# Fused transformer block and mixture of experts: expert weights in DMA runs of four and three slots, and two small reorderings

## The chip, the cores and the metric

The kernel runs on one core of one Trainium2 chip. A NeuronCore has TensorE (PE, matrix products, with weight loads shown apart as PEld), VectorE (DVE), ScalarE (ACT), GpSimd (POOL) and SyncE (SP), which here issues all the DMAs. The metric is the time on the device of one launch, in microseconds, lower is better.

## What is computed

Two blocks follow each other on 256 tokens of width 1024, all in float32. The first has two kinds of attention, a causal depthwise convolution in a gated feed-forward part (width 2816) and a gated embedding. The second has a modulation of its inputs by a condition vector, a convolution, a sparse attention, a pooling mixer and then a mixture of 32 experts. Cut to what the change touches:

```python
h = rms_norm(x, g_pre_ffn[i])
u = causal_depthwise_conv(h @ w_up[i], conv_w[i], conv_b[i])
gate, val = jnp.split(u, 2, axis=-1)
f = (jax.nn.gelu(gate, approximate=True) * val) @ w_down[i]
...
mod = cond @ mod_w[l] + mod_b[l]                     # second block
...
def run(args):                                       # one expert, its tokens
    tok, e = args
    hb = hf[tok]
    return (jax.nn.silu(hb @ w1[e]) * (hb @ w3[e])) @ w2[e]
```

All 32 experts' matrices are read from HBM whatever tokens chose them: each expert has w1, w3 (1024 x 512 each) and w2 (512 x 1024), 6 MB in float32.

## The kernel before

**Weights and the ring.** All large weights pass through `ring`, seven slots of 4096 float32 in each of 128 partitions (2 MB a slot). `STREAM` lists the loads in their order, `PLACE` gives each its slot, round robin in the expert stage, and `BEFORE` names the load that held the slot before. SP walks the stream in that order; ahead of a load it waits (`used`) until the last reader of the old content is done. SP waits in order, so a load that waits holds back those behind it.

**The expert stage.** The experts go in eight groups of four. In a group the four experts stand beside each other in the partitions (32 rows each), so a group has 12 slots of weights: slots 0 to 7 are w1 and w3 (PE products that read `sq`), slots 8 to 11 are w2 (products that read `ar`). Load `j` is slot `j % 12` of group `j // 12`. After slot 7 PE gathers part of the next group's tokens, transposes, and waits for ACT and DVE; after slot 11 DVE takes the result out, PE adds it to the tokens' sums and gathers the rest of the next group's tokens before slot 0 can begin. After group 2, PE also spreads one more row for the end of the kernel.

**Runs.** `RUNS` joins neighbouring loads into one DMA, whose row in a partition is as long as all of them together. From load 19 on the kernel before has runs of two, two and three: loads 19, 21 (two), 23 (three), 26, 28 (two), 30 (three), and so on up to 89 (two), then 91 and 92 singly, and the last ones in parts. A run of two at place 3 (loads 26 + 7i) fills slots 3 and 4, one at place 5 (loads 28 + 7i) slots 5 and 6, and one of three at place 0 (loads 23 + 7i) slots 0 to 2. A run is issued when all of its slots are free, and has one landing: `loaded` gives PE the landing of the whole run for any slot of it.

**The up stage.** `w_up` comes in eleven slabs `j` of eight chunks `k` (512 columns of a partition). Each chunk is split into a rounded part (`hi`, made by ACT) and the rest (`lo`, by DVE, or by POOL for k = 3 and 7), and PE takes 12 products of it. Chunk buffers are four, so ACT can make chunk k when PE has finished chunk k - 4. Between the chunks of slab j, the slab before it is convolved and gated (`conv_step`): ACT makes the base (steps 3 and 4) and the gelu (5), DVE the taps, POOL the product (8), then ACT the product's `hi` and POOL its `lo` (step 9). Step 9 of slab j - 2 stands behind chunk 1 of slab j on ACT and behind chunk 0 on POOL.

**The down stage.** `w_down` is taken in 44 steps in the same way, with the `hi` part on ACT and the `lo` part on DVE. Between these, DVE does one `mod_column` after each of the twelve steps of `DOWN_COLUMNS`, a product and sum of 1024 elements (line 162) with the modulation weights, independent of `w_down`.

Of the kernel before, what the change touches and what calls it, by code (L numbers as in the profile page):

```python
# [57 lines left out]
BEFORE = {x: y for i, x in enumerate(STREAM) for y in [z for z in STREAM[:i] if PLACE[z] == PLACE[x]][-1:]}  # L58


RUNS = {19: 2}
for _i in range(10):
    RUNS.update({21 + 7 * _i: 2, 23 + 7 * _i: 3, 26 + 7 * _i: 2})
RUN_OF = {j: next((a for a in RUNS if a <= j < a + RUNS[a]), j) for j in range(3 * NE)}


# [102 lines left out]
def build(nc, A, out):  # L169
    with ExitStack() as ctx:  # L170
# [61 lines left out]
        def slot(name, j):  # L232
            i = PLACE[name, j]
            return ring[:, i * SLOT:(i + 1) * SLOT]
# [5 lines left out]
        def expert_rows(j):  # L240

            n = RUNS.get(RUN_OF[j], 1)
            o = (j - RUN_OF[j]) * SLOT
            if n == 1:
                return A["exps"][[i for i in range(3 * NE) if RUN_OF[i] not in RUNS].index(j)]
            return A[f"exps{n}"][[i for i in RUNS if RUNS[i] == n].index(RUN_OF[j])][:, o:o + SLOT]

        def expert_run(j):
            n = RUNS[j]
            return A[f"exps{n}"][[i for i in RUNS if RUNS[i] == n].index(j)]  # L250
# [82 lines left out]
        def weight_place(n):  # L333

            buf, o = (fr, WP + 1024 * (n % 4)) if n % 4 < 2 else (fr_h, 1024 * (n % 4 - 2))
            return buf[:, o:o + 512], buf[:, o + 512:o + 1024]
# [10 lines left out]
        def down_src(f, n):  # L347
            return slot("wdown", f // 4)[:, (f % 4) * 1024 + 512 * n:(f % 4) * 1024 + 512 * n + 512]
# [937 lines left out]
        def scalar(act):  # L1286
# [193 lines left out]
            def up_rounded(j, k):  # L1480
                act.wait_ge(loaded("wup", j), pe_up[(8 * j + k - 4) // 8, (k - 4) % 8] if 8 * j + k > 3 else None)
                weight_rounded(8 * j + k, slot("wup", j)[:, 512 * k:512 * k + 512], act_up, "hi", j, k)
# [64 lines left out]
            def conv_step(j, step):  # L1547
                if step == 3:
                    conv_base(j, 0)
                elif step == 4:  # L1550
                    conv_base(j, 1)
                elif step == 5:
                    act.wait_ge(dve_up["conv", j, 0])
                    act.activation(conv_place(j, 0), conv_place(j, 0), ACT.Gelu_apprx_tanh).then_inc(act_up, "gelu", j)
                elif step == 9:
                    act.wait_ge(pool_up["f", j])
                    act.copy(fr[:, FH + 512 * j:FH + 512 * j + 512], conv_place(j, 0)).then_inc(act_up, "f_hi", j)

            for j in range(1, 11):
                for k in range(5 if j == 1 else 0, 8):  # L1560
                    up_rounded(j, k)
                    if j == 1:
                        conv_step(0, k - 2)
                    else:
                        conv_step(j - 1, k)
                        if k == 1:
                            conv_step(j - 2, 9)


# [237 lines left out]
        def vector(dve):  # L1807
# [63 lines left out]
            def mod_column(i):  # L1871

                j, o = i // 4, 1024 * (i % 4)
                dve.wait_ge(loaded("modw", j), act_mod["crow", int(i > 3)])
                if i > 0:
                    dve.wait_ge(dve_mod["column", i - 1])
                t = dve.products_sum(sq[:, 1024:2048], slot("modw", j)[:, o:o + 1024], sq[:, 0:1024], mod[:, i:i + 1]).then_inc(dve_mod, "column", i)
                if i == 15:
                    dve.wait_ge(t)
                    dve.tensor_tensor(mod[:, 0:16], mod[:, 0:16], col("mod_b", 0, 16), ALU.add).then_inc(dve_mod, "first")  # L1880
# [212 lines left out]
                    input_rest(k - 1)  # L2093
            up_rest(0, 7)

            DOWN_COLUMNS = (13, 15, 18, 20, 23, 25, 28, 30, 33, 35, 38, 40)


            def conv_tap(j, p, d):
# [32 lines left out]
            for i, (f, n) in enumerate(DOWN_ORDER):  # L2132
                hi, lo = weight_place(i)
                dve.wait_ge(act_down["hi", f, n])
                dve.tensor_tensor(lo, down_src(f, n), hi.bitcast(F32), ALU.subtract).then_inc(dve_down, "lo", f, n)
                if i in DOWN_COLUMNS:
                    mod_column(4 + DOWN_COLUMNS.index(i))
                if i == 4:
# [285 lines left out]
        def gpsimd(pool):  # L2424
# [34 lines left out]
            def rest(signal, key, src, hi, lo, t, ready):  # L2459
                pool.wait_ge(t, ready)  # L2460
                return pool.tensor_tensor(lo, src, hi.bitcast(F32), ALU.subtract).then_inc(signal, *key)
# [16 lines left out]
            for j in range(1, 11):  # L2478
                for k in range(8):
                    if ("lo", j, k) in POOL_UP:  # L2480
                        t = rest(pool_up, ("lo", j, k), slot("wup", j)[:, 512 * k:512 * k + 512], *weight_place(8 * j + k), t,
                                 act_up["hi", j, k])
                    if j > 1 and k == 0:
                        t = conv_step(j - 2, 9, t)
                t = conv_step(j - 1, 8, t)
            t = conv_step(9, 9, t)
# [359 lines left out]
        @block.scalar  # L2846
        def _(e):
            p = Program(e)
            scalar(p)
            when_flagged(p, over_scalar)  # L2850

        @block.gpsimd
        def _(e):
            gpsimd(Program(e))
# [137 lines left out]
```

## Time and profile before

| what | value |
|---|---|
| median of 3 runs | 911.45 us (911.08 to 913.74) |
| the profiled execution | 911.76 us |
| its span, first to last instruction | 910.0 us |
| PE busy | 757.1 us, 83% of the span |
| DVE busy | 414.5 us, 46% |
| ACT busy | 337.4 us, 37% |
| share of the chain that ended last | PE 51%, DMA 31%, DVE 12% |
| moved by DMA | 299.01 MB, of which the expert weights are 201 MB (96 slots) |

The page divides the span into 40 slices of 22.75 us. Up to slice 23 the PE row shows 9 in each; then, in the expert stage, it falls to 4 to 7 and the DMA row rises to 9 in each. "Chain that ended last" follows the last instruction back through what released it; it tells which engine the time belongs to, but a DMA's share in it includes the time that the DMA stood behind another in the queue.

### The profile page before, as it was taken

The page shows a single profiled execution, that of the slowest core. Times are in us where ns is not written, and L with a number is a line of the kernel's source. Part 1 is how long each engine was busy: PE and PEld are TensorE (multiplying, and loading weights), DVE is VectorE, ACT ScalarE, POOL GpSimd, SP SyncE. Part 2 cuts the span into 40 slices and gives each one's busy share as a digit, 9 for nine tenths or more (in the row PEclk, how much of TensorE's full clock was granted, in tenths as well). Part 3 has the DMA queues.
Part 4 walks back from the last instruction along what each step waited for, and adds up shares of the span by engine and source line. Part 5 has one row for each costly group of instructions (what it writes and reads, how often), then busy time and mean ns, then how long its engine had stood idle before and what let it go on. Part 6 is the DMA issues. An engine that isn't in the chain of part 4 may idle for free.

```text
span 910.0 us, 12726 instructions
## 1 busy us (share of the span) xinstructions
PE 757.1 (83%) x5292; PEld 524.8 (58%) x5292; DVE 414.5 (46%) x851; ACT 337.4 (37%) x664; POOL 136.5 (15%) x136
## 2 busy tenths in 40 slices
PE   9999999999999999999999984567574575665575
PEld 7986589999998877898786431123221222212223
DVE  5777777899998975899613110010100100001002
ACT  5766667666666667824723110001000000000012
POOL 0011043544431334103010000000000000000000
PEclk9999999999999999999999997789888888888888
DMA  9958964455553982646968999999999999999995
GB/s 352 423 209 315 427 243 162 185 186 185 186 185 108 387 340 79 266 175 236 341 256 328 431 444 424 427 433 431 432 428 431 435 432 429 431 442 418 433 423 242
DMA packets 19648, 299.01 MB, mean 329 GB/s; under 512 B 2176, under 2 KB 2560, under 8 KB 6144
## 3 DMA queue, kind: packets, MB, share of 16 engines
q1 hardware_dynamic: 19584, 298.13, 79.9%
q8 instruction: 43, 0.70, 0.3%
q14 instruction: 21, 0.17, 0.1%
HBM read 297.08 MB, written 1.05 MB: 328 GB/s over the span
## 4 chain that ended last, share of the span: by engine, by line
PE 51%; DMA 31%; DVE 12%; ACT 4%; issue 1%; POOL 0%; SPq 0%; DVEq 0%; POOLq 0%
PE ps L114 51%; DMA ring<-in_exps 31%; DVE ar L140 3%; DVE fr L132 2%; DVE sq L162 1%; DVE fr_h L132 1%; DVE yT L140 1%; ACT L120 1%; ACT yT L120 1%; PE ps L117 1%; DVE hT L140 0%; DVE ar L132 0%; ACT ar L123 0%; ACT sq L120 0%; ACT ar L120 0%
## 5 line engine op out<-in xcount | busy, mean ns | idle before, releaser
L114 PE MATMUL ps<-fr 128*128 128x256 f32 (+2 forms) x1332 | 213.3, 316 | 1.6 <-DVE fr L132 0.8
L114 PEld LDWEIGHTS ps<-fr 128*128 128x128 f32 (+1 forms) x1332 | 187.3, 189 | 21.0 <-DVE fr L132 2.7
L114 PE MATMUL ps<-ring,sq 128*32 128x512 f32 x936 | 127.6, 697 | 78.3 <-DMA ring<-in_exps 78.3
L114 PE MATMUL ps<-ring,ar 128*32 128x512 f32 (+4 forms) x784 | 87.8, 573 | 52.4 <-DMA ring<-in_exps 48.4
L114 PEld LDWEIGHTS ps<-ring,sq 128*32 128x32 f32 x936 | 31.4, 125 | 165.6 <-DMA ring<-in_exps 91.9
L132 DVE TENSOR_TENSOR ar<-ar,ps 128x512 f32<-128x512 f32 x9 | 6.2, 688 | 241.5 <-PE ps L114 240.2
L132 DVE TENSOR_TENSOR fr<-ring,fr 128x512 fp32r<-128x512 f32 (+2 forms) x119 | 92.5, 804 | 12.0 <-ACT fr L123 11.7
L123 ACT ACTIVATE fr<-ring 128x512 fp32r<-128x512 f32 (+2 forms) x143 | 84.7, 623 | 33.5 <-PE ps L114 30.4
L114 PEld LDWEIGHTS ps<-ring,ar 128*32 128x32 f32 (+1 forms) x784 | 26.3, 120 | 99.6 <-issue 45.6
L123 ACT ACTIVATE ar<-ps 128x512 f32<-128x512 f32 (+4 forms) x48 | 27.2, 570 | 151.8 <-PE ps L117 131.4
L132 DVE TENSOR_TENSOR ar<-ps,ar 128x512 f32<-128x512 f32 (+6 forms) x38 | 23.4, 632 | 120.7 <-PE ps L114 120.4
L120 ACT ACTIVATE sq<-ps,misc 128x128 f32<-128x128 f32 x31 | 11.9, 456 | 162.7 <-PE ps L114 162.7
L114 PE MATMUL ps<-fr,fr_h 128*128 128x256 f32 x552 | 70.6, 284 | 0.1
L114 PE MATMUL ps<-ar 128*128 128x512 f32 (+10 forms) x328 | 62.3, 407 | 8.1 <-DVE ar L132 6.9
L114 PEld LDWEIGHTS ps<-fr,fr_h 128*128 128x128 f32 x552 | 67.5, 191 | 0.6 <-DVE fr_h L132 0.3
L132 POOL TENSOR_TENSOR ar<-ar 128x128 f32<-128x128 f32 (+2 forms) x21 | 11.2, 533 | 309.7 <-DVE ar L132 308.6
L114 PEld LDWEIGHTS ps<-ar 128*128 128x128 f32 (+4 forms) x328 | 35.5, 168 | 36.9 <-issue 16.7
L123 ACT ACTIVATE fr_h<-ring 128x512 fp32r<-128x512 f32 x66 | 41.5, 633 | 22.2 <-PE ps L114 22.1
L132 DVE TENSOR_TENSOR fr_h<-ring,fr_h 128x512 fp32r<-128x512 f32 x43 | 46.2, 1083 | 6.8 <-ACT fr_h L123 6.6
L120 ACT ACTIVATE ar<-ps 128x768 f32<-128x768 f32 (+1 forms) x21 | 14.8, 715 | 84.8 <-PE ps L114 83.4
L132 POOL TENSOR_TENSOR fr<-ring,fr 128x512 fp32r<-128x512 f32 x24 | 34.1, 1421 | 66.2 <-ACT fr L123 65.3
L140 DVE SCALAR_TENSOR_TENSOR yT<-ps,cols,yT 128x255 f32<-128x255 f32 (+1 forms) x88 | 37.2, 475 | 4.6 <-ACT yT L120 4.6
(193 smaller groups left out, 918.0 us busy)
## 6 DMA issues: line engine op xcount, KB each, us to landing
ring<-in_exps SPq DMA_DIRECT2D x21, 4096.0 KB, 28.5
ring<-in_exps SPq DMA_DIRECT2D x10, 6144.0 KB, 26.9
ring<-in_modw SPq DMA_DIRECT2D x12, 2048.0 KB, 8.9
ring<-in_exps SPq DMA_DIRECT2D x12, 2048.0 KB, 10.1
ring<-in_wup SPq DMA_DIRECT2D x11, 2048.0 KB, 12.3
ring<-in_wdown SPq DMA_DIRECT2D x5, 2048.0 KB, 7.9
ring<-in_win SPq DMA_DIRECT2D x4, 2048.0 KB, 11.8
ring<-in_exps SPq DMA_DIRECT2D x8, 1024.0 KB, 10.4
```

The lines of the kernel that those rows point to most:

```text
L114: return Issue(self.e and self.e.matmul(o, l, r, start=start, stop=stop, skip_group_check=True))
L117: return Issue(self.e and self.e.transpose(o, i, ident))
L120: return Issue(self.e and self.e.activation(o, i, f, **kw))
L123: return Issue(self.e and self.e.activation(o, i, ACT.Copy, scale=scale))
L132: return Issue(self.e and self.e.tensor_tensor(o, a, b, op))
L140: return Issue(self.e and self.e.scalar_tensor_tensor(out=o, in0=a, scalar=s, in1=b, op0=op0, op1=op1))
L162: return Issue(self.e and self.e.tensor_tensor_reduce(out=o, in0=a, in1=b, scale=1.0, scalar=0.0, op0=ALU.mult, op1=ALU.add, accum_out=total))
```

## The change

Three edits:

1. `RUNS`: loads 19, 21 and 23 stay as they are (two, two, three). From load 26 on, the two runs of two become one run of four (26 + 7i, slots 3 to 6), nine times, between the runs of three (30 + 7i, slots 0 to 2). The last run of two (89) and all that is behind it stay. Row length of a run of four is 64 KiB in a partition, and its array in HBM is laid out for it.
2. Step 9 of slab 0 (the product's `hi` on ACT and `lo` on POOL), in slab 2 alone, stands behind chunk 3 instead of chunk 1 (ACT) and chunk 0 (POOL).
3. Three of the twelve `mod_column` stand at other steps of the down stage: 13 becomes 14, 15 becomes 16, 38 becomes 37.

```diff
-RUNS = {19: 2}
-for _i in range(10):
-    RUNS.update({21 + 7 * _i: 2, 23 + 7 * _i: 3, 26 + 7 * _i: 2})
+RUNS = {19: 2, 21: 2, 23: 3, 89: 2}
+for _i in range(9):
+    RUNS.update({26 + 7 * _i: 4, 30 + 7 * _i: 3})
...
                         conv_step(j - 1, k)
-                        if k == 1:
+                        if k == (3 if j == 2 else 1):
                             conv_step(j - 2, 9)
...
-            DOWN_COLUMNS = (13, 15, 18, 20, 23, 25, 28, 30, 33, 35, 38, 40)
+            DOWN_COLUMNS = (14, 16, 18, 20, 23, 25, 28, 30, 33, 35, 37, 40)
...
-                    if j > 1 and k == 0:
+                    if j > 1 and k == (3 if j == 2 else 0):
                         t = conv_step(j - 2, 9, t)
```

SP in the expert stage (a `-` row is before, a `+` row is now; 8192 elements are two slots, 12288 three, 16384 four; `pe_exp` is PE's signal that a slot has been read):

```order
 L166 DMA ring<-in_exps 128x8192 [waits pe_exp] x2
 L166 DMA ring<-in_exps 128x12288 [waits pe_exp]
-L166 DMA ring<-in_exps 128x8192 [waits pe_exp] x2
+L166 DMA ring<-in_exps 128x16384 [waits pe_exp]
 L166 DMA ring<-in_exps 128x12288 [waits pe_exp]
```

Each pair of two-slot loads has become one load that waits for the readers of all four slots; the three-slot loads stand where they stood.

PE at loads 33 to 36, slots 9, 10 and 11 of group 2 and what follows them (`ring3_in` and `ring5_in` are the landings at places 3 and 5):

```order
 L114 MATMUL ps<-ring,ar 32x512 x7
 L114 MATMUL ps<-ring,ar 32x512 [waits ring3_in]
-L114 MATMUL ps<-ring,ar 32x512 x15
-L114 MATMUL ps<-ring,ar 32x512 [waits ring5_in]
-L114 MATMUL ps<-ring,ar 32x512 x7
+L114 MATMUL ps<-ring,ar 32x512 x23
 L114 MATMUL ps<-ar 128x512 [waits dve_exp]
 L114 MATMUL ps<-ar 128x512
```

The products are the same; the wait for place 5 is gone, since the wait ahead of slot 9 is now for all four.

ACT in slab 2 (`fr` and `fr_h<-ring` are `hi` parts of chunks, `fr<-yT` is step 9 of slab 0, `yT<-ps,cols` the base of slab 1):

```order
 L120 ACTIVATE yT<-yT 128x512
 L123 ACTIVATE fr<-ring 128x512 x2
-L123 ACTIVATE fr<-yT 128x512
-L123 ACTIVATE fr_h<-ring 128x512 x2
-L120 ACTIVATE yT<-ps,cols 128x256 x2
+L123 ACTIVATE fr_h<-ring 128x512 x2
+L120 ACTIVATE yT<-ps,cols 128x256 x2
+L123 ACTIVATE fr<-yT 128x512
 L123 ACTIVATE fr<-ring 128x512
```

Chunks 2 and 3 and the base have come ahead of step 9.

## Rows read from the trace of the kernel before

**Rows 1.** Page, DMA's busy tenths in 40 slices of the span.

```profile
DMA  9958964455553982646968999999999999999995
```

**Rows 2.** Busy time by stretch: us, engines (instructions), PEclk, DMA share, GB/s.

```profile
550.00:870.00 320.00, 195.40 (x1306) 71.41 (x1310) 21.66 (x52) 16.07 (x36) 3.98 (x10) 0.82 1.00 431
...
611.90:615.60 3.70, 3.61 (x16) 0.59 (x16) 0.00 (x0) 0.00 (x0) 0.00 (x0) 0.50 1.01 438
```

**Rows 3.** Chain that ended last, from 520 us on: shares by line.

```profile
by line: DMA ring<-in_exps 72.6%; PE ps L114 23.8%; issue 0.4%; ACT sq L120 0.4%; DVE sq L140 0.4%; DVE ar L132 0.4%; DVE sq L137 0.4%; ACT hT L120 0.2%; SPq L166 0.1%; ACT misc L120 0.1%; SPq L111 0.1%; DVE misc L143 0.1%
```

**Rows 4.** Timeline of PE, evenly fed stretch: start, us, what, [idle before, releaser].

```profile
807.44 5.28 PE L114 MATMUL ps<-ring,sq 128*32 128x512 f32 x32 [2.98 <-DMA ring<-in_exps]
817.15 5.34 PE L114 MATMUL ps<-ring,sq 128*32 128x512 f32 x32 [4.43 <-DMA ring<-in_exps]
831.68 3.39 PE L114 MATMUL ps<-ring,sq 128*32 128x512 f32 x16 [9.19 <-DMA ring<-in_exps]
...
838.61 7.07 PE L114 MATMUL ps<-ring,ar 128*32 128x512 f32 x64 [0.90 <-DVE sq L137]
```

**Rows 5.** Timeline of PE, loads 30 to 42, around the end of group 2.

```profile
592.44 5.26 PE L114 MATMUL ps<-ring,sq 128*32 128x512 f32 x32 [9.20 <-DMA ring<-in_exps]
...
601.25 5.36 PE L114 MATMUL ps<-ring,ar 128*32 128x512 f32 x48 [0.90 <-DVE sq L137]
611.99 3.64 PE L114 MATMUL ps<-ring,ar 128*32 128x512 f32 x16 [5.39 <-DMA ring<-in_exps]
...
624.67 7.21 PE L114 MATMUL ps<-ring,sq 128*32 128x512 f32 x64
637.04 5.15 PE L114 MATMUL ps<-ring,sq 128*32 128x512 f32 x32 [5.17 <-DMA ring<-in_exps]
```

**Rows 6.** Timeline of SP: issues of loads 37, 40, 42 and 56.

```profile
603.28 0.33 SPq L166 DMA_DIRECT2D ring<-in_exps  x1
...
606.70 0.33 SPq L166 DMA_DIRECT2D ring<-in_exps  x1
...
626.71 0.33 SPq L166 DMA_DIRECT2D ring<-in_exps  x1
...
686.29 0.33 SPq L166 DMA_DIRECT2D ring<-in_exps  x1
```

**Rows 7.** DMA issue at 603.28: count, KB, us from issue to landing.

```profile
ring<-in_exps SPq DMA_DIRECT2D x1, 6144.0 KB, 23.2
```

**Rows 8.** Timeline of PE, loads 47, 51 and 54.

```profile
671.01 3.52 PE L114 MATMUL ps<-ring,ar 128*32 128x512 f32 x16 [2.97 <-DMA ring<-in_exps]
...
695.26 6.77 PE L114 MATMUL ps<-ring,sq 128*32 128x512 f32 x48 [9.07 <-DMA ring<-in_exps]
705.32 5.15 PE L114 MATMUL ps<-ring,sq 128*32 128x512 f32 x32 [3.29 <-DMA ring<-in_exps]
```

**Rows 9.** DMA issues from 384 to 423 us, each with nothing in flight.

```profile
ring<-in_exps SPq DMA_DIRECT2D x4, 2048.0 KB, 7.9
```

**Rows 10.** Timeline of slab 2 of the up stage, POOL, ACT and PE.

```profile
157.81 2.18 POOL L132 TENSOR_TENSOR yT<-yT 128x512 f32<-128x512 f32 x1 [0.29 <-DVE yT L140]
...
160.03 0.63 ACT L123 ACTIVATE fr<-yT 128x512 fp32r<-128x512 f32 x1 [2.15 <-POOL yT L132]
...
162.80 3.04 PE L114 MATMUL ps<-fr,fr_h 128*128 128x256 f32 x24
...
166.65 3.13 PE L114 MATMUL ps<-fr 128*128 128x256 f32 x24 [0.81 <-DVE fr L132]
...
169.87 3.14 PE L114 MATMUL ps<-fr,fr_h 128*128 128x256 f32 x24
```

**Rows 11.** Timeline of the down stage, PE and DVE.

```profile
285.10 3.02 PE L114 MATMUL ps<-fr_h,fr 128*128 128x512 f32 x12 [0.17 <-DVE fr_h L132]
...
323.75 1.52 PE L114 MATMUL ps<-fr_h,fr 128*128 128x512 f32 x6
...
282.11 2.31 DVE L162 CUSTOM_DVE_ANT_0 sq<-ring,sq 128x1024 f32<-128x1024 f32 x1
```

## The prediction, made before the changed kernel ran

> **What bounds the kernel now.** I read the 40 slices first, to see where DMA is full [rows 1], then the table by stretch for the expert stage, the chain, and the timelines of PE and SP there. From 550 to 870 us the DMA engines are busy all the time, share 1.00 at 431 GB/s, while PE is busy 195.4 of 320 us [rows 2]; the chain from 520 us on is DMA for 72.6% and PE for 23.8% [rows 3]. The stage is a pipe of fixed rate that never runs dry. Its end moves by three things alone: by when it starts, by its bytes and their rate, and by any time in which no load is queued. Ahead of it, DMA is full only in places [rows 1], PE and the elementwise engines set the time, and what they save moves the start of the pipe.
>
> **The pipe's prices.** PE waits for each load, so its starts are landings. A load of two slots takes 817.15 - 807.44 = 9.71 us, one of three 831.68 - 817.15 = 14.53 us [rows 4]. The difference, 4.82 us, is one slot; 2 x 4.82 = 9.64, so a DMA costs 0.07 us beside its bytes. A load of four should take 4 x 4.82 + 0.07 = 19.35 us. A load into an empty queue lands 7.9 us after its issue for one slot [rows 9]: 7.9 - 4.82 = 3.1 us more than the bytes. While another load is in flight this 3.1 us is hidden; when the queue has run dry it is paid. PE's prices: the first slot after an idle time runs at a granted clock of 0.50, 1.2 GHz, for 3.61 us [rows 2], the next ones take 1.71 us each (603.28 to 606.70, two slots) [rows 6]. A pair after an idle time is thus 5.3 us [rows 5].
>
> **Edit 1, fewer DMAs.** Nine DMAs fall away: -9 x 0.07 = -0.6 us. No row of 64 KiB is in the trace, the longest is 48 KiB; if the row is cut into two of 32 KiB, the gain is 0, and I keep 0 to -0.6.
>
> **Edit 1, the queue.** Before, while PE reads a landed run of two, a run of two and one of three are still in flight, 9.71 + 14.53 = 24 us of transfers behind which the reading hides. Now the ring holds one run of four (A) and one of three (B). While PE reads A, only B is in flight, 14.53 us. The next A is issued when all four slots are read. To keep the pipe full PE has to read A within 14.53 - 3.1 = 11.4 us of its landing. For the nine A's this is:
>
> - Four slots with nothing between (loads 26, 40, 61, 68, 75): 3.6 + 3 x 1.71 = 8.8 us. It fits.
> - Load 33 (slots 9, 10, 11 of group 2, then slot 0 of group 3): before, slot 11 begins at 611.99 [rows 5], and the load that waits for slot 0 is issued at 626.71 [rows 6], 14.72 us, the first 3.6 us of it being slot 11 at the low clock. Now two slots stand ahead, the first of them pays for the low clock, so 3.42 us are added: 18.2 us. That is 6.8 us too late (18.2 - 11.4).
> - Load 47 (slot 11 of group 3, then 0, 1, 2): slot 11 begins at 671.01 [rows 8], the issue that waits for slot 2 is at 686.29 [rows 6]: 15.3 us, 3.9 too late.
> - Load 54 (slots 6, 7, then 8, 9 of group 4): slot 7 at the low clock to the start of slot 8 takes 838.61 - 831.68 = 6.93 us [rows 4]; one slot more ahead and two behind add 3 x 1.71 and 0.3 for the signals: 12.4 us, 1.0 too late.
> - Load 82 (10, 11, then 0, 1) has the same boundary, but behind it stands B and then load 89 of two slots, which waits for 82 and 83 only, 5.3 us. It fits, and the loads of one slot behind it have 24 us.
>
> The B runs have 19.35 us of transfer to hide in: the worst, load 58 (10, 11, then 0), needs 3.6 + 1.7 + 8.3 = 13.6 us, where 8.3 is 15.3 - 3.6 - 2 x 1.71. They fit. So the pipe runs dry three times, for 6.8 + 3.9 + 1.0 = +11.7 us. The cover that is gone is the second two-slot load; nothing else covers it. Behind the waiting four-slot load SP has only the next B, whose slots PE reads after A's, so it is not delayed by this.
>
> **A correction.** The wait ends with the slowest of the 16 rings, and in a full pipe its lag grows: the load issued at 603.28 lands 23.2 us later, at 626.5 [rows 6, 7], and the two-slot load behind it at 637.04 [rows 5], 10.5 us for what costs 9.71; 705.32 - 695.26 [rows 8] is 10.06. An empty queue lets that ring catch up, so some 1.0 us of the 0.8 + 0.35 is not paid: -1.0 us (0 to -2).
>
> **The bound from below.** If the 3.1 us is itself partly such lag, a dry queue costs less. With 2.0 instead (the landing would then be that of an unlagged ring) the three are 5.7, 2.8 and 0: 8.5 us. The rows of 384 to 423 us are empty queues, as here, so I take 3.1 and keep 8.5 for the range.
>
> **Edit 2.** ACT stands idle for 2.15 us until POOL has made slab 0's product, and only then rounds chunks 2 and 3 [rows 10]. PE's groups of 24 start every 2.88 us where nothing waits; here 166.65 - 162.80 = 3.85 and 169.87 - 166.65 = 3.22, together 1.3 us lost. With step 9 behind chunk 3, ACT is bound by PE's release of buffers, the chunks are ready a good 1 us sooner and the loss is gone; step 9 lands in ACT's and POOL's idle time, and its readers are in the down stage and in slab 2's base, a slab later. POOL's `lo` of chunk 3 goes ahead of step 9, which helps. -1.2 us (0 to -1.3).
>
> **Edit 3.** The column at 282.11 takes 2.31 us and stands before the rest that PE waits for at 285.10 [rows 11]; at 2.72 us for 12 products the start should be at 284.76. Behind step 14 it stands after that rest: -0.4 us. The other end, step 38 to 37: the group before 323.75 starts at 320.59, so it takes 3.16 where 2.72 is the rule, 0.44 us; the DVE work ahead of it is the same in sum, the order differs, so -0.44 to +0.4, and I take -0.1. No DMA waits longer, since each slot's last column keeps its step.
>
> **The sum.** Against the profiled 911.76 us: -0.6 + 11.7 - 1.0 - 1.2 - 0.4 - 0.1 = +8.4, 920.2 us. That execution is 0.3 above the median of 911.45, so against the median: **919.8 us**.
>
> **A page against this sum.** In sentences of its own: the Trainium skill, "SBUF — State Buffer", section "The DMA setup-cost knee", says to join loads into the largest single transfer, because each pays a fixed cost of about 2 us. By that figure, as an estimate, nine DMAs less would give 18 us. The trace agrees for an empty queue (3.1 us), and not in the full pipe (0.07 us).
>
> **The rivals.**
>
> - *Each DMA carries its fixed cost in the pipe too*: then nine fewer give 9 x 3.1 = 28 us back, 911.45 - 28 + 11.7 - 1.7 = 893. The spacing of 9.71 and 14.53 us leaves no room for it [rows 4]. Chance 0.01. (It is what the page's rule would make of it.)
> - *The pipe does not run dry* (faster): the margin of 11.4 us is enough, because PE passes the group boundaries sooner when fed from four landed slots. It decides at 18.2 and 15.3 us falling below 11.4. Then the gains stand alone: 911.45 - 1.7 - 0.6 = 909.2. Against it: both numbers are PE's own work and its waits for DVE and ACT, with the weights landed already. Chance 0.05.
> - *It runs dry, but cheaply*: 8.5 us or less, clock higher at the landing (1.9 us less for each), lag given back in full: 8.5 - 2 - 1.7 - 0.6 = +4.2, 915.7; with the clock too, 912. Chance 0.14, of which 0.05 is within 0.3%.
> - *The 64 KiB rows are slower* than the bytes say, by some 3% of 9 x 19.35 us: +5 us on the forecast, 925. Against it, rows of 32 and 48 KiB have the same rate. Chance 0.06.
> - *The forecast*, three dry times at 3.1 us: 917.5 to 922.5, chance 0.74.
>
> **How the numbers follow.** The predicted time is the likeliest case's. The range for 8 in 10 takes in most of the cheap case: 915.7 to 923.0. A measurement here tells 0.3% (2.7 us) from no change. Same: 0.05 of the cheap case and 0.01 of the second rival (dry once, for a moment), 0.06. Faster: 0.01 + 0.04 = 0.05. Slower: 0.89.
>
> **What would show it.** In the profile after: SP's issue of load 40 about 18.2 us after load 33's landing and that of load 54 15.3 us after 47's; DMA's share under 1.00 in the slices around 625 and 700 us, 1.00 elsewhere; four-slot loads landing 19.35 us behind the one before them where the queue is full; PE's groups in slab 2 every 2.88 us; PE's first wait in the expert stage some 1.7 us earlier. I am wrong if load 40 is issued before 626 us, if four-slot loads take other than 19.3 us, or if the share is 1.00 throughout.

## The result, and the profile after

| what | before | changed |
|---|---|---|
| median of 4 runs each, same chip | 912.17 us (911.08 to 913.74) | 925.07 us (924.56 to 926.51) |
| ratio of medians, 95% interval | | 1.0142 (1.0129 to 1.0155) |
| the profiled execution | 911.76 us | 924.56 us |
| its span | 910.0 us | 922.8 us |
| PE busy | 757.1 us | 756.4 us |

The changed kernel is slower by 12.9 us, 1.4%. (All ratios here and below leave out three executions of 1130 to 1873 us, which stand far off from all others of their kernels.) The direction and the place were forecast, the size was not: 8.4 us were forecast, and 925.07 lies above the range, which ended at 923.0. PE is busy for the same time in both, so the 12.8 us between the two profiled executions are waiting.

The page of the changed kernel, DMA's busy tenths in 40 slices of 23.07 us, which answers to [rows 1]:

```profile
DMA  9958963444455883638789999996998999999996
```

Counted from 0, slice 27 (623 to 646 us) and slice 30 (692 to 715 us) have fallen below 9. By stretch (us, then busy time and instructions of PE, PEld, DVE, ACT, POOL, then PEclk, DMA share, GB/s), which answers to [rows 2]:

```profile
550.00:620.00 70.00, 42.47 (x254) 13.97 (x254) 4.61 (x11) 2.70 (x6) 0.80 (x2) 0.73 1.00 427
624.00:634.00 10.00, 9.30 (x84) 5.14 (x86) 0.00 (x0) 2.59 (x6) 0.00 (x0) 1.00 0.33 110
634.00:700.00 66.00, 31.40 (x214) 11.56 (x210) 4.07 (x10) 2.70 (x6) 0.80 (x2) 0.74 0.99 429
700.00:706.00 6.00, 6.00 (x62) 1.82 (x56) 0.00 (x0) 0.60 (x1) 0.00 (x0) 1.00 0.53 175
736.00:742.00 6.00, 3.90 (x40) 1.18 (x36) 0.00 (x0) 0.00 (x0) 0.00 (x0) 1.00 0.84 314
```

Three holes, where the prediction put them: the DMA engines move nothing for 10 x 0.67 = 6.7 us, 6 x 0.47 = 2.8 us and 6 x 0.16 = 1.0 us. In the stretches between, the share is 0.99 to 1.00. The chain that ended last (start, us, what; [rows 3] is its sum by line before) shows what happens around each hole. Before, it ran down the DMA queue; now it changes to PE wherever a load of four waits for its slots:

```profile
586.88 24.51 DMA ring<-in_exps
...
611.44 8.00 PE ps L114 x48
...
619.46 0.70 DVE ar L132
...
620.30 5.47 PE ps L114 x24
...
625.79 1.51 ACT sq L120 x4
...
627.35 3.06 PE ps L114 x24
...
630.49 23.11 DMA ring<-in_exps
...
687.68 0.04 issue
687.73 3.69 PE ps L114 x16
...
703.15 22.83 DMA ring<-in_exps
...
738.58 22.80 DMA ring<-in_exps
```

Load 33 lands at 611.40. PE reads its four slots with the end of group 2 between them, and load 40 is issued at 630.49: 19.1 us of reading, 18.2 forecast. The load in flight behind it, 37, landed at 626.5 (issued at 603.30, 23.2 us to its landing). So load 40 lands at 653.60, 27.06 us behind load 37, where a full queue gives 19.35: +7.7 us. For load 54, 703.15 - 687.68 = 15.5 us of reading (15.3 forecast), and it lands 23.77 us behind load 51: +4.4. For load 61, 738.58 - 725.98 = 12.6 us (12.4), and 20.87 us: +1.5. Together +13.6 us, where the sum has 11.7. The third hole shows that the queue need not be empty for this: load 61 is issued 1.9 us before load 58 lands (738.58 and 740.51), and that is less than the 3 us by which a load has to be ahead. The time by which each load is late is longer than the time without any transfer, 13.6 us against 10.5. Most of the rest is in the first packet of each ring after a hole, which the trace's packets show to take 3.1 to 3.2 us where the others take 2.42. (A load comes as 128 packets, one for each partition, eight on each of 16 rings.)

Where the queue is full, loads of four cost what was forecast. The timeline of PE (start, us, what, [idle before, releaser]):

```profile
557.51 3.64 PE L114 MATMUL ps<-ring,ar 128*32 128x512 f32 x16 [10.89 <-DMA ring<-in_exps]
...
576.86 1.08 PE L114 MATMUL ps<-ring,sq 128*32 128x512 f32 x4 [4.06 <-DMA ring<-in_exps]
...
829.51 9.85 PE L114 MATMUL ps<-ring,sq 128*32 128x512 f32 x64 [12.48 <-DMA ring<-in_exps]
844.04 3.64 PE L114 MATMUL ps<-ring,sq 128*32 128x512 f32 x16 [4.67 <-DMA ring<-in_exps]
...
863.46 6.51 PE L114 MATMUL ps<-ring,ar 128*32 128x512 f32 x32 [8.04 <-DMA ring<-in_exps]
```

576.86 - 557.51 = 19.35 us for four slots, 844.04 - 829.51 = 14.53 for three, 863.46 - 844.04 = 19.42 for four. Rows of 64 KiB run at the rate of rows of 32 and 48 KiB. The loss is nowhere in the transfers.

The first of these rows also dates the start of the stage: load 23 is waited for until 557.51; in the kernel before, the same group of products starts at 558.48. That is 0.97 us earlier, where the small edits had a forecast of 1.7. This is one execution of each, and such a difference needs care: the seven kernels of this document that have edits 2 and 3 in full are alike up to this place, and load 23 lands in them at 556.8 to 558.8 us.

### The profile page after: what moved, and what is told of

The parts are those of the page before. It is cut to its first block, busy times and chain, and to the rows that moved or that the text cites. A ratio compares the mean times of both kernels' runs of the same rounds, so it can differ in the third digit from the quotient of the medians.

```text
span 922.8 us, 12717 instructions
## 1 busy us (share of the span) xinstructions
PE 756.4 (82%) x5292; PEld 525.6 (57%) x5292; DVE 415.4 (45%) x851; ACT 337.6 (37%) x664; POOL 137.6 (15%) x136
## 4 chain that ended last, share of the span: by engine, by line
PE 55%; DMA 29%; DVE 11%; ACT 4%; issue 1%; SPq 0%; DVEq 0%
PE ps L114 55%; DMA ring<-in_exps 28%; DVE ar L140 3%; DVE fr L132 2%; DVE sq L162 1%; DVE fr_h L132 1%; ACT L120 1%; DMA ar<-in_pT 1%; DVE ar L132 1%; PE ps L117 1%; DVE hT L140 0%; ACT yT L120 0%; ACT ar L123 0%; ACT sq L120 0%; ACT ar L120 0%
## 5 line engine op out<-in xcount | busy, mean ns | idle before, releaser
L114 PE MATMUL ps<-ring,sq 128*32 128x512 f32 x936 | 122.8, 678 | 80.6 <-DMA ring<-in_exps 80.6
L132 DVE TENSOR_TENSOR fr<-ring,fr 128x512 fp32r<-128x512 f32 (+2 forms) x119 | 93.1, 810 | 12.9 <-ACT fr L123 12.6
L114 PE MATMUL ps<-ar 128*128 128x512 f32 (+10 forms) x328 | 64.6, 415 | 8.0 <-DVE ar L132 6.9
L114 PEld LDWEIGHTS ps<-ar 128*128 128x128 f32 (+4 forms) x328 | 36.5, 172 | 38.3 <-issue 18.2
L132 DVE TENSOR_TENSOR fr_h<-ring,fr_h 128x512 fp32r<-128x512 f32 x43 | 49.8, 1166 | 4.8 <-ACT fr_h L123 3.9
## 6 DMA issues: line engine op xcount, KB each, us to landing
ring<-in_wup SPq DMA_DIRECT2D x11, 2048.0 KB, 12.4
```

The lines of the kernel that those rows point to most:

```text
L114: return Issue(self.e and self.e.matmul(o, l, r, start=start, stop=stop, skip_group_check=True))
L132: return Issue(self.e and self.e.tensor_tensor(o, a, b, op))
```

## The experiments

Each ratio is to the kernel before, run on the same chip in turn with it, with a 95% interval. Numbers of the profile are from one execution of each kernel.

### Each edit alone

First, which edit the time belongs to. `e1_runs_only` has the first edit alone, `e2_up_only` the second, `e3_columns_only` the third, `e4_up_col38` the second and the two columns 13 to 14 and 15 to 16, with 38 left where it was and the loads as before.

```diff
# e1_runs_only: the RUNS of the change, nothing else
# e2_up_only: k == (3 if j == 2 else 1), k == (3 if j == 2 else 0)
# e3_columns_only
-DOWN_COLUMNS = (13, 15, 18, 20, 23, 25, 28, 30, 33, 35, 38, 40)
+DOWN_COLUMNS = (14, 16, 18, 20, 23, 25, 28, 30, 33, 35, 37, 40)
# e4_up_col38: as e2, and
+DOWN_COLUMNS = (14, 16, 18, 20, 23, 25, 28, 30, 33, 35, 38, 40)
```

> Runs of four and three alone, the up and down stages as before. Theory A (the pipe runs dry three times, as read in the profile after: the load spacings of 27.1, 23.8 and 20.9 us in place of 19.35, less the lag that before had there): the whole loss is in this edit, and without the 1.0 us by which the expert stage starts earlier in the changed kernel the time is 925.1 + 1.0 = 926 us, +1.5% on before. Rival B (edits 2 and 3 carry part of the loss by a cost of their own in the second half): this kernel is nearer to before than the changed one, 918 to 923 us.

> Slab 0's step 9 behind chunk 3 in slab 2, nothing else. Theory: PE's groups in slab 2 start every 2.88 us, 1.3 us are gained there (the changed kernel shows 184.45 -> 183.09), and this shift is carried to the start of the expert stage: -1.3 us, 910.8. Rival: the late down stage (DVE and POOL side by side on the last weights) gives it back, since DVE there is no longer ahead of PE: -0.5 us or less.

> The three modulation columns moved, nothing else. Theory A: steps 13 and 15 to 14 and 16 give 0.47 us, step 38 to 37 costs 0.9 us (the changed kernel loses that much of its lead between 312 and 321 us): +0.4 us, 912.6. Rival B: 37 costs something only when PE is ahead by edit 2; then -0.5 us, 911.7. PE's group starts between 310 and 324 us tell the two apart.

> Edit 2, and of edit 3 only 13 to 14 and 15 to 16; the column at 38 stays, and the runs are those of before. Theory A (the move to 37 is what loses 0.9 us): PE leaves the down stage 1.84 us earlier than before, less the 0.44 us that before lost there too: about -1.8 us, 910.3. Rival B (DVE beside POOL bounds the end of the down stage, whichever step the column has): the lead falls to about 1.0 us as in the changed kernel, 911.1.

| kernel | median | ratio to before |
|---|---|---|
| e1_runs_only | 924.04 | 1.0144 (1.0126 to 1.0162) |
| e2_up_only | 911.64 | 0.9995 (0.9986 to 1.0004) |
| e3_columns_only | 912.52 | 1.0002 (0.9992 to 1.0011) |
| e4_up_col38 | 910.52 | 0.9985 (0.9975 to 0.9996) |

The median of before was 912.43. **The whole loss is in the first edit**: +1.44% alone, +1.42% with the others. The loads in `e1_runs_only` also repeat the three late ones: 27.16, 23.94 and 20.91 us behind the load before. The medians of the small edits are within 0.8 us of before, each alone, and their intervals (-1.3 to +0.4 us, -0.7 to +1.0) hold zero as well as what was expected of them, so their times decide nothing. Their rows say more. In `e2_up_only`, PE's timeline in slab 2 (before, [rows 10]):

```profile
162.44 3.04 PE L114 MATMUL ps<-fr,fr_h 128*128 128x256 f32 x24
165.31 3.04 PE L114 MATMUL ps<-fr 128*128 128x256 f32 x24
```

A group every 2.88 us, and the next at 168.19: both stalls are gone. PE reaches 322.09 at the end of the down stage for 323.75 before [rows 11], 1.66 us ahead. In the changed kernel the lead is 0.98 us (322.77). It is 1.78 us when the group at 310.65 starts, and is lost in the next three. First two of the changed kernel's groups, then the same two of `e8_late_pairs`, a kernel of a later section whose down stage has the same edits:

```profile
313.73 3.04 PE L114 MATMUL ps<-fr 128*128 128x512 f32 x12 [0.20 <-DVE fr L132]
317.18 3.03 PE L114 MATMUL ps<-fr_h,fr 128*128 128x512 f32 x12 [0.41 <-DVE fr_h L132]
```

```profile
313.37 2.88 PE L114 MATMUL ps<-fr 128*128 128x512 f32 x12
316.09 2.92 PE L114 MATMUL ps<-fr_h,fr 128*128 128x512 f32 x12
```

The obvious suspect is the column that was moved from step 38 to 37, which in the changed kernel's DVE timeline stands ahead of the second wait:

```profile
314.21 1.21 DVE L162 CUSTOM_DVE_ANT_0 sq<-ring,sq 128x1024 f32<-128x1024 f32 x1
...
315.35 2.38 DVE L132 TENSOR_TENSOR fr_h<-ring,fr_h 128x512 fp32r<-128x512 f32 x2
```

But the first wait, at 313.73, is ahead of that column, and `e8_late_pairs` has the column at the same step and loses nothing: PE starts the group at 310.65 there too, and the last one at 322.00, 1.75 us ahead of before. DVE is simply earlier by 0.50 us there (its column starts at 313.71). Going back from there, the two kernels part at ACT, where the changed kernel waits for the landing of `in_pT`, the input of the gated embedding:

```profile
298.39 0.63 ACT L123 ACTIVATE fr<-ar 128x512 fp32r<-128x512 f32 x1 [0.50 <-DMA ar<-in_pT]
```

That load took 6.2 us from issue to landing, for 5.3 to 5.7 in the kernels in which nothing waits for it. Of the 14 profiles only two have this wait, the changed kernel (0.50 us) and `e5_fours_plain` (0.85 us), and just these two are slow behind it: from the group at 310.65, or its like, to the last one takes 12.12 and 12.32 us. In the other six with column 37 it takes 11.26 to 11.35, in those with column 38 11.24 to 11.45, before included. **So the 0.8 us of lead go with a load that landed late in this execution, and none of it is shown to be the column's.** (Whether such a landing would cost less with the column at 38 no profile shows.) Both theories of `e3_columns_only` had given the column a price, with a lead or without, and its own rows show none: its first two columns bring PE from 0.46 us behind before, at 282.50, to level at 287.94, and it is still level at the last group (323.74). `e4_up_col38` starts the last group at 321.95, a lead of 1.80 us. It is 1.4 us faster than before (0.4 to 2.3), though against `e2_up_only` the intervals overlap.

### Which run of four is the costly one

The loads 26, 40, 61, 68 and 75 have four slots that PE reads in one go; 33, 47 and 54 have a group's boundary among theirs. I meant to show that the cost sits at the latter, with fours at one kind only and pairs elsewhere (both kernels with the second and third edit).

```diff
+RUNS = {19: 2, 21: 2, 23: 3, 89: 2}
+for _i in range(9):
+    RUNS.update({26 + 7 * _i: 4, 30 + 7 * _i: 3} if 26 + 7 * _i in FOURS
+                else {26 + 7 * _i: 2, 28 + 7 * _i: 2, 30 + 7 * _i: 3})
# e5_fours_plain:    FOURS = (26, 40, 61, 68, 75)
# e6_fours_boundary: FOURS = (33, 47, 54)
```

> Edits 2 and 3 as in the changed kernel, but runs of four only where no boundary of a group or of its halves lies inside (loads 26, 40, 61, 68, 75); at 33, 47, 54 and 82 two runs of two. Theory A (a run of four costs only where PE cannot read it in 11.4 us): no dry time, five DMAs less, the 1.0 us start: 912.2 - 1.0 - 0.3 = 910.9 us, DMA share 1.00 throughout. Rival B (each run of four costs, by its late landing or its 64 KiB rows): 5/9 of the loss stays, about 919.

> The counterpart: runs of four only at loads 33, 47 and 54, two runs of two elsewhere; edits 2 and 3 as in the changed kernel. Theory A: the three dry times stand as in the changed kernel, 7.7 + 4.4 + 1.5 us less the lag, 924.5 to 925.5 us. A small part may go: the run of four before load 33 (load 26) is read in pairs, so the low clock is shorter there. Rival B: 3/9 of the loss, about 916.

`e5_fours_plain`: 917.85 us, ratio 1.0051 (1.0032 to 1.0071). `e6_fours_boundary`: 914.09 us, 1.0015 (1.0005 to 1.0024). **Both expectations missed, and in opposite directions.** The chain of `e5_fours_plain`:

```profile
611.35 3.69 PE ps L114 x16
...
615.90 7.61 PE ps L114 x24
...
628.23 23.24 DMA ring<-in_exps
```

The load issued at 628.23 is 40, a plain four. It waits for slots 33 to 36, of which 35 and 36 land at 611.31, and their reading with the boundary takes 16.9 us, the first 9 of them at a granted clock of 0.50; it lands 25.63 us behind load 37, 6.3 us too late. In `e6_fours_boundary`, load 40 is a pair, which waits for slots 33 and 34 alone and is issued at 616.98, in time, though 33 is a four. Only load 54 is late there, a four that waits for the four at 47:

```profile
679.50 3.64 PE L114 MATMUL ps<-ring,ar 128*32 128x512 f32 x16 [11.05 <-DMA ring<-in_exps]
...
717.91 5.00 PE L114 MATMUL ps<-ring,sq 128*32 128x512 f32 x32 [17.97 <-DMA ring<-in_exps]
```

It lands 23.89 us behind load 51, 4.5 too late. (Less the 1.2 us that the small edits and three DMAs fewer bring, 3.3 us should be left; 1.4 were measured, 0.5 to 2.2. In the profile 2.7 us are there when load 86 lands, 868.42 for 865.72. From there to the end it takes 43.5 us for 44.3 before; no edit touches this part, and it differs from 43.5 to 45.8 us among the 14 profiles. The rest is between the profiled execution and the median.) That is the prediction's own mechanism, which I had applied wrongly in these two expectations: a load is late by the reading of the slots that it waits for, whatever it brings itself.

### Late issue, late landing, and the clock

A run of four does two things: its slots come as one landing, so the reading of the first begins later, and its issue waits for the last of four slots. `e8_late_pairs` has the second alone: the runs of before, but loads 40, 54 and 61, pairs, wait until all four slots are read (with the second and third edit). `e7_warm` is the changed kernel with products of the identity into an unused part of PSUM ahead of PE's waits for loads 33 and 47, 32 and 50 of them, which leave PE's own work as it was and keep PE busy up to the landing.

```diff
# e8_late_pairs
-                    for i in range(j, j + RUNS[j]):
+                    for i in range(j, j + (4 if j in (33 + 7, 47 + 7, 54 + 7) else RUNS[j])):
                         sp.wait_ge(*used(*BEFORE[name, i]))
# e7_warm, on the changed kernel
                     j = 12 * g + 8 + k
+                    if j in (33, 47):
+                        pe.wait_ge(dve_exp["st", g])
+                        for _ in range({33: 32, 47: 50}[j]):
+                            pe.matmul(bank(1, 256, 384), ident, ident, True, True)
                     pe.wait_ge(expert_in(j))
```

> The changed kernel with idle products (identity by identity into an unused part of a bank) ahead of PE's waits for loads 33 and 47, 32 and 50 of them, so that PE is busy until just before the landing. Theory A (the mis-sized term was PE's clock: after the longer idle time it stays at 0.50 for 5 to 6 us and not 3.6): the granted clock is 1.00 when these loads land, PE reads load 33's four slots and passes the boundary in 16.3 in place of 19.1 us, load 47's in 13.5 in place of 15.4; the two dry times shrink by 2.8 and 1.9 us: 925.1 - 4.7 = 920.4. Rival B (the time from landing to issue is set by DVE, ACT and PE's pipeline, not the clock): no change, 925.

> Runs of two, two and three as before, edits 2 and 3 in, but SP issues the first pair of loads 40, 54 and 61 only when all four slots are read (as a run of four would), then the second pair at once. It parts the two things that a run of four does: issuing late, and landing late. Theory A (both together make the loss, since PE starts reading only when the fourth slot has landed): the pair 33 lands 9.7 us before the pair 35, PE is 14.7 us behind the latter's landing at its issue, so only load 40 is late, by 14.7 + 3.1 - 14.5 = 3.3 us, loads 54 and 61 are in time: 912.2 - 1.0 + 3.3 - 1.0 (lag given back) = 913.5. Rival B (the late issue alone is the cause): as the changed kernel, 925.

`e7_warm`: 919.58 us, ratio 1.0083 (1.0063 to 1.0103), as expected. What the clock did at load 33 in the changed kernel (first four lines), and then in `e7_warm` (the extra products, then the first 3 us after the landing):

```profile
611.40:613.40 2.00, 1.96 (x12) 0.60 (x16) 0.00 (x0) 0.00 (x0) 0.00 (x0) 0.50 0.91 393
613.40:615.40 2.00, 2.00 (x12) 0.40 (x8) 0.00 (x0) 0.00 (x0) 0.00 (x0) 0.50 0.91 393
615.40:617.40 2.00, 2.00 (x16) 0.52 (x12) 0.00 (x0) 0.00 (x0) 0.00 (x0) 0.67 1.01 426
617.40:619.50 2.10, 1.99 (x20) 0.36 (x12) 0.04 (x1) 0.00 (x0) 0.00 (x0) 1.00 1.08 468
```

```profile
603.49 7.41 PE L114 MATMUL ps<-con 128*128 128x128 f32 x64
611.84 4.50 PE L114 MATMUL ps<-ring,ar 128*32 128x512 f32 x40 [0.94 <-DMA ring<-in_exps]
```

```profile
611.80:614.80 3.00, 2.96 (x28) 0.94 (x32) 0.00 (x0) 0.00 (x0) 0.00 (x0) 1.00 0.98 426
```

After an idle time of 8.24 us PE ran at 0.50, 1.2 GHz, for some 5 us, and was at 1.00, 2.4 GHz, from 617.4 on. The prediction had one slot, 3.6 us, at the low level [rows 2]. With PE kept busy, the granted clock is 1.00 from the landing on, slots 9 to 11 take 5.40 us for 8.00, and load 40 is issued 16.4 us after load 33's landing for 19.1. The chain of `e7_warm` from there:

```profile
628.23 21.74 DMA ring<-in_exps
...
698.85 21.83 DMA ring<-in_exps
```

Loads 40, 54 and 61 land 23.81, 20.99 and 19.70 us behind the load before: 4.5 + 1.6 + 0.3 = 6.4 us too late for 13.6. But not all of that is won, since the loads right behind these three now come 15.83, 15.77 and 15.67 us later for 14.53, which they did not in the changed kernel. PE's waits for loads 54 and 58:

```profile
720.72 4.93 PE L114 MATMUL ps<-ring,sq 128*32 128x512 f32 x32 [15.63 <-DMA ring<-in_exps]
...
736.50 5.34 PE L114 MATMUL ps<-ring,ar 128*32 128x512 f32 x32 [3.67 <-DMA ring<-in_exps]
```

With them it is 10.1 us for 13.6. The times of the kernels say 0.83% for 1.42%, that is 5.4 us less of 12.9 (with both intervals some 3 to 8), and the reading ahead of loads 40 and 54 is 2.7 and 1.8 us shorter. **Some 40% of the loss, between a quarter and 60%, is what the low clock adds to the reading.** The rest is PE's work at full clock and its waits for DVE and ACT at the boundary. (Load 54's reading, ahead of 61, was not kept at the high clock here.)

`e8_late_pairs`: 917.52 us, ratio 1.0054 (1.0038 to 1.0071), 4 us above what was expected. Its executions differ: the profiled one took 914.13, the others 917.4 to 918.0. In the profiled one, of loads 40, 54 and 61 only 40 is late:

```profile
610.21 3.37 PE L114 MATMUL ps<-ring,ar 128*32 128x512 f32 x16 [4.27 <-DMA ring<-in_exps]
...
624.73 5.36 PE L114 MATMUL ps<-ring,sq 128*32 128x512 f32 x48 [0.17 <-DMA ring<-in_exps]
638.28 6.40 PE L114 MATMUL ps<-ring,sq 128*32 128x512 f32 x32 [8.19 <-DMA ring<-in_exps]
```

638.28 - 624.73 = 13.55 us, where a pair takes 9.71: +3.8. Slot 11 is read at the low clock, and the issue is 14.5 us after its landing. The remaining 3.4 us of the other executions no profile shows. That the clock can make such a difference is shown by `e5_fours_plain`, which reads the same slots 35 and 36 here: after an idle time of 4.74 us its granted clock is 0.50 for 9 us and the reading takes 16.9 us, where `e8_late_pairs`, after 4.27 us, has 0.50 for 3 us and takes 14.5. `e12_late_pairs_warm` asks whether those 3.4 us are the clock's: `e8_late_pairs` with 17 such extra products ahead of the wait for load 35.

```diff
# on e8_late_pairs
                     j = 12 * g + 8 + k
+                    if j == 35:
+                        pe.wait_ge(dve_exp["st", g])
+                        for _ in range(17):
+                            pe.matmul(bank(1, 256, 384), ident, ident, True, True)
                     pe.wait_ge(expert_in(j))
```

> The kernel with the late pairs, with 17 idle products on PE ahead of its wait for load 35, so that PE's clock is high when 35 lands. Its profiled execution took 914.1 us, its others 917.4 to 918.0; the profile of the kernel with runs of four at the plain places shows the same reading of 35 and 36 at 16.9 us in place of 14.5 because the clock came back later. Theory A (the clock's return is what differs): with the clock high the reading takes 12.6 us in every execution, load 40 is late by 12.6 + 3.5 - 14.5 = 1.6 us, and all executions agree at 912.5 us within 1. Rival B (something else differs between executions): they still spread by 3 us.

913.63 us, ratio 1.0017 (1.0008 to 1.0027), with its executions between 912.8 and 914.7. The loads stand like this:

```profile
611.25 1.92 PE L114 MATMUL ps<-ring,ar 128*32 128x512 f32 x16 [0.29 <-DMA ring<-in_exps]
...
625.77 5.36 PE L114 MATMUL ps<-ring,sq 128*32 128x512 f32 x48 [1.69 <-DMA ring<-in_exps]
637.69 5.50 PE L114 MATMUL ps<-ring,sq 128*32 128x512 f32 x32 [6.56 <-DMA ring<-in_exps]
```

Slot 11 takes 1.92 us for 3.37, load 40 is 11.92 - 9.71 = 2.2 us late for 3.8, and by the ratios 3.4 us are back. The profiles account for 1.6 of these. That the rest is a later return of the clock in the executions that were not profiled is likely, and not shown: the two kernels ran on different chips, each beside its own runs of before.

Late issue alone is thus 4.5 us over before in the median, of 12.9, and 0.9 us with the clock kept high. Two questions are left: whether late landing is harmless alone, and whether a chain of fours has the whole cost.

### Fours that free a pair, fours that free a four

`e10_fours_free` has fours only where the load that waits for a four is a pair: 26, 33, 47, 68, 75, 82 (68, 75 and 82 stand in a row, but had no dry time in the changed kernel), and the small edits of `e4_up_col38`. `e9_fours_chained` has the five fours 33, 40, 47, 54, 61, and the second and third edit. `e11_up_col38_again` is `e4_up_col38` on another chip.

```diff
# e10_fours_free:    FOURS = (26, 33, 47, 68, 75, 82)
# e9_fours_chained:  FOURS = (33, 40, 47, 54, 61)
```

> Runs of four at loads 33, 40, 47, 54 and 61, two runs of two elsewhere; edits 2 and 3 as in the changed kernel. The traces so far say that a run of four is late by what the slots it replaces take to be read, so late are loads 40, 54 and 61, not 33, 47 and 54 as I had put it for the two mixed kernels. Theory A: each late load is in here together with the run of four ahead of it, so the whole loss is: 923.5 to 925.5 us, with load spacings of 27, 24 and 21 us at 40, 54 and 61. Rival B (each of the nine costs something): 5/9 of the loss, about 920.

> Runs of four at the other six places, 26, 33, 47, 68, 75 and 82, none of which waits for a boundary; two runs of two at 40, 54 and 61. Slab 2's step 9 moved, columns at 14, 16 and 38. Theory A: no dry time, spacing 19.35 us at each of the six, six DMAs less (-0.4 us), else as the kernel with the same two edits and the old runs: 910.1 us. Rival B (late landings or 64 KiB rows cost by themselves): over 912.

> Slab 2's step 9 moved and the columns at 14, 16 and 38, runs as before, once more beside the kernel with six runs of four: 910.5 us. If the first result was chance, 911.5 or more.

| kernel | median | ratio to before (912.72) |
|---|---|---|
| e9_fours_chained | 923.18 | 1.0113 (1.0098 to 1.0128) |
| e10_fours_free | 914.64 | 1.0013 (1.0004 to 1.0023) |
| e11_up_col38_again | 910.51 | 0.9980 (0.9971 to 0.9989) |

`e9_fours_chained` has 10.3 us of the loss (8.9 to 11.7) with five fours; in its profiled execution, which at 926.1 us was its longest, loads 40, 54 and 61 come 28.32, 23.93 and 21.12 us behind the ones before them. The medians leave 2.6 us for the other four fours, the intervals 0.8 to 4.5.

`e10_fours_free` missed: 4.1 us over `e11_up_col38_again`, where a small gain was expected. PE and the clock around load 47:

```profile
678.66 3.64 PE L114 MATMUL ps<-ring,ar 128*32 128x512 f32 x16 [12.05 <-DMA ring<-in_exps]
683.20 5.77 PE L114 MATMUL ps<-ar 128*128 128x512 f32 x8 [0.91 <-DVE ar L132]
...
706.14 6.19 PE L114 MATMUL ps<-ring,sq 128*32 128x512 f32 x32 [4.95 <-DMA ring<-in_exps]
```

```profile
678.60:681.60 3.00, 2.94 (x16) 0.59 (x16) 0.00 (x0) 0.00 (x0) 0.00 (x0) 0.50 1.10 475
681.60:684.60 3.00, 2.10 (x6) 0.84 (x3) 1.69 (x4) 0.00 (x0) 0.40 (x1) 0.50 0.95 410
684.60:687.60 3.00, 3.00 (x5) 1.09 (x4) 0.00 (x0) 0.00 (x0) 0.40 (x1) 0.53 0.98 426
```

Load 54, a pair, waits for slots 47 and 48. They landed at 678.62 with the whole four, slot 11 and the boundary are read at 0.50 for almost 9 us, and the issue is at 692.72, 14.1 us behind the landing, for a cover of 14.53 - 3.5 = 11.0. It lands 3.3 us late. So late landing alone can dry the queue too (in this one execution; the kernel was not run with the clock kept high), and "a four is free if a pair waits for it" holds only where there is no boundary among the first two slots.

## Why the prediction was right about the place and wrong about the size

The profile's 12.8 us against the sum of 8.4, step by step:

| step | forecast | measured |
|---|---|---|
| start of the stage (edits 2 and 3) | -1.7 | -0.97 (one execution) |
| dry times at loads 40, 54, 61 | +6.8 +3.9 +1.0 = +11.7 | +7.7 +4.4 +1.5 = +13.6 |
| nine DMAs fewer | -0.6 | -0.6 (a load of four 19.35 to 19.42) |
| lag of the slowest ring given back | -1.0 | +0.2 (what is left over up to load 86) |
| from load 86's landing to the end | 0 | +0.6 |
| sum | +8.4 | +12.8 |

- **What holds.** The mechanism, its three places and their order of size; one landing of B as the only cover; 19.35 us for four slots; no price for rows of 64 KiB; the runs 26, 68, 75 and 82 free. `e1_runs_only` and `e9_fours_chained` show the same three late loads at nearly the same spacings. That an empty queue is three times 3 us, and not a fixed cost for each DMA, is decided by `e1_runs_only`: nine DMAs fewer alone are +1.44%.
- **The dry times, short by 1.9 us.** Two terms were mis-sized. The reading is 0.9 us longer at load 33 and 0.2 at each of the others: the prediction let the clock come back with the second slot, after 3.61 us, as in the one row that it used; here the low level lasted some 5 us. (In `e1_runs_only`, where it lasted some 4, the same reading took 18.5 us. Four slots read in one go, forecast at 8.8 us, took 9.7 to 9.9 at loads 26, 61, 68 and 75 and 9.0 at load 40, which cost nothing where they had 11 us.) The restart is 22.8 to 23.1 us from issue to landing, 3.5 to 3.8 more than 19.35, where rows of loads into an empty queue in another stage [rows 9] had given 3.1. The packets in the traces part this. In all three restarts the first packet starts 0.95 us after the issue, the first sixteen take 3.1 to 3.2 us each for 2.42, the slowest of the 16 rings ends 1.1 to 1.5 us behind the middle one, and the landing is told 0.4 to 0.5 us after that. In the four loads of [rows 9] the first packet is as soon and the first sixteen lose as much (0.5 to 0.9 us), but the slowest ring is 0.6 to 0.9 us behind and the landing is told 0.2 to 0.4 us later: the ring is most of the difference. Less 0.6 us, since load 37 itself landed late in its place, 15.14 us behind load 33 for 14.53.
- **The lag, wrong by 1.2 us.** I took off 1.0 for a slowest ring that catches up in an empty queue. This step fails: at the end of the restarted loads 40, 54 and 61 the slowest ring is 1.5, 1.1 and 1.1 us behind the middle one, as it is in a full queue (0.9 to 1.8 us in the other loads of the stage). So the lag is inside the restart and nothing is given back. Only in `e7_warm` was it 0.3 us, at loads 40 and 54, which makes its restarts 21.74 and 21.83 us; and there the next load came 15.8 us behind for 14.53, so that it was paid one load later. The correction came from two rows of before, and 0 was the end of its range to take.
- **Edits 2 and 3, 0.7 us less than forecast.** Edit 2's stalls are gone, 1.36 us, and so is the stall at 285.10. PE is 1.78 us ahead of before at 310.65, which is the forecast. The 0.8 us that go after it belong to the late landing of `in_pT` in this execution, as shown above, and not to the column at 37, whose term (-0.1) no run contradicts. The forecast had nothing for differences between executions.
- **The end, 0.6 us.** The last products of w2 in groups of 32 take 3.03 us (902.74, granted clock 0.62) where the same group before took 1.93 (891.14, granted clock 1.00). This follows from no edit. From load 86's landing to the end the 14 profiles have 43.5 to 45.8 us, before 44.3 and the changed kernel 44.9, so 0.6 us lie within what executions differ by.
- **The rivals.** The first rival, a fixed cost that each DMA carries in the pipe too (893), is refuted by `e1_runs_only`. The cheap dry queue (8.5 us, lag given back) was the wrong side of the middle: each of its assumptions went the other way. The rival with 64 KiB rows gives the right number, 925, by a cause that its own rows refute. The range had 3.2 us above the forecast, and the four differences are 1.9 + 1.2 + 0.7 + 0.6 = 4.4, all to one side. The first two, 3.1 us, are errors of the working: low clock, restart and lag were each sized from the most favourable or the only row, and the range upward had the 64 KiB rival in it but none of these. The other two, 1.3 us, are chance as far as the profiles tell.

**The better kernel** is `e4_up_col38`: the loads as before, step 9 of slab 0 behind chunk 3, columns 13 and 15 at 14 and 16, column 38 left. 910.5 us on two chips, 1.4 and 1.8 us under before (intervals 0.4 to 2.3 and 1.0 to 2.6), and some 14 us under the changed kernel. That 38 is a better step than 37 is not shown: edits 2 and 3 in full with the old loads were not run, and the stage takes as long with either.

What stays open: why the low clock lasts so differently, and with it the 3.4 us between executions of `e8_late_pairs`; and why the slowest ring was not slow in the two restarts of `e7_warm`.

## What to carry to other kernels

Count for every load of a ring what is still in flight while it waits, and hold against it the time from the landing of what it waits for to its last reader, at the clock that PE has after its idle time and with whatever stands between the slots. Joining loads makes both worse, the cover shorter and the wait longer, and in a full queue it saves 0.07 us for each DMA: the rule to join loads that the prediction weighed (the Trainium skill, "SBUF — State Buffer", "The DMA setup-cost knee") is made for loads that each pay the fixed cost, as by the 3.1 us of [rows 9] in an empty queue, and not for this one. And before a difference of under 1 us between two profiles is given to an edit, the same stretch should be looked at in every other profile that has the edit: the column at step 37 looked like the cause in one, and five with the same down stage show no cost.

## What the runs showed of the hardware that I had not expected

- The time at a granted clock of 0.50 after an idle PE differed much, and not by the length of the idle time: 3.6 us after 5.4 us of it [rows 2, 5], 3 us after 4.3 in `e8_late_pairs` but 9 us after 4.7 at the same loads in `e5_fours_plain`, some 5 us after 8.2 us (load 33; some 4 us at the same place in `e1_runs_only`), almost 9 us after 12 us in `e10_fours_free`, but only 4 us after 18.1 us (load 40 in the changed kernel: 0.50 from 653.6 to 657.6, then 0.98; four slots in 9.04 us). In the two cases of 9 us, PE also waited for DVE in that time. It is read from single executions. Idle products up to the landing kept it at 1.00 in the places where they were tried.
- The restart of an empty queue took 3.5 to 3.8 us over the bytes in the changed kernel and 2.4 to 2.5 us at loads 40 and 54 in `e7_warm` (21.74 and 21.83 less 19.35). Nearly the whole difference is the slowest of the 16 rings, 1.1 to 1.5 us behind the middle one there and 0.3 us here.
- DVE's rests of 512 elements take 0.68 us each alone and up to 1.8 us while POOL makes a rest beside them. In the changed kernel two of DVE's take 2.38 us from 315.35 on, and POOL's one runs from 314.87 for 1.71 us.
